# Odd attention: next position's first scores ahead of the last value products, output products beside the last positions, and a new order at both ends

## The reference

```python
for i in range(DEPTH):
    m = even_mixer(...) if i % 2 == 0 else odd_mixer(...)
    x = layer_norm(DEEPNORM_ALPHA * x + m, ln_mix_g[i], ln_mix_b[i])
    f = conv_ffn(x, w_up[i], conv_w[i], conv_b[i], w_down[i])
    x = layer_norm(DEEPNORM_ALPHA * x + f, ln_ffn_g[i], ln_ffn_b[i])
```

```python
z  = q @ k.T                                   # -inf where key >= query
sp = maximum(z, 0) + log1p(exp(-abs(z)))
a  = exp(z - (sum of sp from this key on to the query))
o  = a @ v
```

## Time and profile before

| | |
|---|---|
| median of 3 runs | 1261.15 us (1259.26 to 1261.15) |
| profiled execution | 1259.06 us, span 1257.2 us |
| TensorE busy | 1223.0 us, 97% of the span |
| VectorE, ScalarE, GpSimd busy | 630.4, 507.8, 554.2 us |
| odd attention, positions 0 to 7 | from 702.46 to 843.32 us |
| even attention, positions 0 to 7 | from 75.10 to 234.08 us |

### The profile page before, as it was taken

One profiled execution on the slowest core, in us unless ns is written; L12 is line 12 of the kernel. 1 busy time (PEld: TensorE's weight loads), 2 busy tenths in 40 slices (PEclk: granted clock), 3 DMA queues, 4 the chain that ended last, 5 costly groups with the idle time before them and its releaser, 6 DMA issues.

```text
span 1257.2 us, 17097 instructions
## 1 busy us (share of the span) xinstructions
PE 1223.0 (97%) x6274; PEld 1005.9 (80%) x6274; DVE 630.4 (50%) x992; ACT 507.8 (40%) x747; POOL 554.2 (44%) x242
## 2 busy tenths in 40 slices
PE   9999998999999999999999999989999999999996
PEld 8877776789888888888788777768988888888885
DVE  2045666276556665511370465553766666652226
ACT  3245565344333333322232556553533333342223
POOL 4534444343444444455614333314344444444553
PEclk9999999999999999999999999999999999999998
DMA  7221212123222222222222111112132222223211
GB/s 292 101 84 59 92 59 93 39 97 135 100 100 81 88 98 100 100 101 100 100 101 103 67 68 67 38 63 101 68 133 82 88 97 100 100 100 101 100 67 67
DMA packets 20022, 117.25 MB, mean 93 GB/s; under 512 B 2448, under 2 KB 2832, under 8 KB 7568
## 3 DMA queue, kind: packets, MB, share of 16 engines
q1 hardware_dynamic: 18400, 112.21, 24.8%
q10 hardware_dynamic: 1584, 4.51, 1.1%
HBM read 110.41 MB, written 2.10 MB: 89 GB/s over the span
## 4 chain that ended last, share of the span: by engine, by line
PE 87%; DVE 6%; ACT 3%; POOL 2%; issue 2%; DVEq 0%; ACTq 0%
PE bank L888 50%; PE bank L857 28%; POOL w_lo L244 2%; PE bank L940 2%; PE bank L967 1%; PE bank L954 1%; DVE probs L729 1%; PE bank L1024 1%; ACT w_hi L301 1%; PE bank L1005 1%; PE bank L1013 1%; PE bank L832 1%; DVE x L573 1%; DVE ln_mul L593 1%; DVE x L617 1%
## 5 line engine op out<-in xcount | busy, mean ns | idle before, releaser
L244 POOL TENSOR_TENSOR w_lo<-w_raw,w_hi 128x1024 fp32r<-128x1024 f32 x196 | 505.1, 2599 | 617.1 <-ACT w_hi L301 608.9
L888 PE MATMUL bank<-xt_hi,w_hi 128*128 128x512 f32 (+1 forms) x1056 | 397.0, 376 | 2.9 <-ACT v_all L331 1.7
L888 PE MATMUL bank<-xt_lo,w_hi 128*128 128x512 f32 (+1 forms) x1056 | 396.7, 376 | 0.0
L888 PE MATMUL bank<-xt_hi,w_lo 128*128 128x512 f32 (+1 forms) x1056 | 392.9, 372 | 0.0
L301 ACT ACTIVATE w_hi<-w_raw 128x2048 fp32r<-128x2048 f32 x97 | 185.3, 1910 | 208.5 <-PE bank L857 204.7
L888 PEld LDWEIGHTS bank<-xt_hi,w_hi 128*128 128x128 f32 x1056 | 198.9, 188 | 39.5 <-ACT v_all L331 2.4
L888 PEld LDWEIGHTS bank<-xt_lo,w_hi 128*128 128x128 f32 x1056 | 198.8, 188 | 39.1 <-issue 4.8
L888 PEld LDWEIGHTS bank<-xt_hi,w_lo 128*128 128x128 f32 x1056 | 198.7, 188 | 34.0
L857 PE MATMUL bank<-w_hi,a_hi 128*128 128x512 f32 x480 | 151.7, 396 | 2.9 <-POOL w_lo L244 1.9
L857 PE MATMUL bank<-w_hi,a_lo 128*128 128x512 f32 x480 | 149.0, 390 | 0.0
L857 PE MATMUL bank<-w_lo,a_hi 128*128 128x512 f32 x480 | 148.8, 390 | 0.0
(11 more groups left out here) (90 smaller groups left out, 1156.9 us busy)
## 6 DMA issues: line engine op xcount, KB each, us to landing
w_raw<-w_stream SPq DMA_DIRECT2D x97, 1024.0 KB, 4.8
x<-x_in SPq DMA_DIRECT2D x4, 512.0 KB, 7.1
gain<-ln_in ACTq DMA_DIRECT2D x4, 512.0 KB, 4.2
shift<-ln_in ACTq DMA_DIRECT2D x4, 512.0 KB, 6.3
qs<-qc SPq DMA_DIRECT2D x16, 128.0 KB, 2.1
ks<-kc SPq DMA_DIRECT2D x16, 128.0 KB, 2.0
out<-x SPq DMA_DIRECT2D x3, 512.0 KB, 2.6
w_raw<-w_stream SPq DMA_DIRECT2D x2, 512.0 KB, 5.9
```

Of the source, the lines that this page charges most:

```text
L244: pool.tensor_tensor(w_lo[slot(c)][:, part], w_raw[s][:, part], w_hi[slot(c)][:, part].bitcast(F32), ALU.subtract).then_inc(lo_ready, 1)
L888: mm = pe.matmul(out_bank[:, tok], w, m, start=n == 0, stop=n == len(todo) - 1)
```

## The change

1. `odd_position` of positions 0 to 6 sends `scores(0)` and `scores(1)` of the next position right behind its own `weigh(2)`, ahead of two fills, `weigh(3)` and the rest. They wait there for the next position's query and key. Position 0 alone (`first`) sends its own at its start. `share` becomes (10, 11, 15, 8, 2), so that all key products stand in front of `turn(2)`.
2. `odd_body` on ScalarE: the cast moves from the front of the position to behind `weight_part(0)`; the copy of the next keys moves from the end to ahead of `weight_part(3)`. On VectorE `break_stick(1)` goes ahead of `turn_out(0)`.
3. The output products of the first two steps are divided anew between the positions and what follows. Even layer: 6 in position 6, 30 in position 7, 60 behind (before: 0, 24, 72). Odd layer: 0, 48, 48. They now reach token tile 3 (banks 6 and 7) and need the bank that position 6 leaves, so a wait for `ot_lo` stands in front of it (`bank_free`). In odd position 7 all transposes use bank 4 (`turn_bank`), each waiting for the copy of the one before.
4. At the start VectorE makes the second token tile's remainder before it copies the second half of the first weights. In the last norm the last half's sum goes ahead of tile 2's value update.

The core of the diff (in `norm_out`, `norm` and `norm_last` the calls of `norm_root` are only written elsewhere, except for what point 4 says; `even_position` takes the same `filler` and `first` as the odd one):

```diff
@@ ScalarE, odd_body
-                for j in range(4):
-                    if j == 2 and before:
-                        out_heads(a, i - 1, (c - 1) % 2)
-                    if j == 0:
-                        heads(b + AT_QK + c + 2, it)
...
+                soft_part(0)
+                soft_part(1)
+                weight_part(0)
+                heads(b + AT_QK + c + 2, it)
+                if before:
+                    out_heads(a, i - 1, (c - 1) % 2)
+                weight_part(1)
+                soft_part(2)
+                turn_out(a, 1, 4 * i + 1, dense)
...
+                soft_part(3)
+                weight_part(2)
                 if dense:
                     act.wait_ge(w_used, b + AT_QK + i + 2)
                     act.activation(ka[(c + 1) % 2][:, :], bank[1][:, :], ACT.Copy).then_inc(a["k_ok"], 1)
+                weight_part(3)
+                turn_out(a, 3, 4 * i + 3, dense)
@@ TensorE, odd_position
-                share = (10, 11, 14, 9, 2) if dense else (6,) * 4 + (0,)
+                share = (10, 11, 15, 8, 2) if dense else (11, 11, 13, 9, 4)
...
-                    if j >= 2:
+                    if j >= 2 and dense:
                         pe.wait_ge(a["tev_v"] if j % 2 == 0 else a["tev_a"], 2 * i + j // 2)
+                    if j >= 1 and not dense:
+                        pe.wait_ge(a["tev_a"] if j % 2 == 0 else a["tev_v"], 2 * i + (j - 1) // 2 + 1)
...
+                if first:
+                    pe.wait_ge(a["q_ok"], i + 1)
+                    pe.wait_ge(a["k_ok"], i + 1)
+                    scores(0)
+                    scores(1)
...
                 weigh(2)
+                if dense:
+                    pe.wait_ge(a["q_ok"], i + 2)
+                    pe.wait_ge(a["k_ok"], i + 2)
+                    scores(0, 1 - par)
+                    scores(1, 1 - par)
                 fill(share[NT])
                 weigh(3)
@@ TensorE, even_position
-                share = (8, 8, 9, 9, 9, 3) if dense else (4, 4, 5, 5, 5, 1)
+                share = (8, 8, 9, 9, 9, 3) if early else (8, 8, 8, 3, 3) if dense else (3, 5, 7, 7, 6)
@@ TensorE, the layer
+                def bank_free(t, n, g):
+                    a = A[l]
+                    if (t, g) == (0, 0) and l == 0:
+                        pe.wait_ge(a["q_cp"], NPOS)
+                    if t == 3:
+                        pe.wait_ge(a["ot_lo"], NPOS - 1 + g)
...
+                if l == 0:
+                    beside = [(0, 0, 0)], [(0, 0, 1), (3, 0, 0), (0, 1), (3, 1, 0)]
+                    rest = [(1, 0), (2, 0), (3, 0, 1), (1, 1), (2, 1), (3, 1, 1)]
+                else:
+                    beside = [], [(0, 0), (2, 0, 1), (3, 0, 0), (0, 1), (2, 1, 1), (3, 1, 0)]
+                    rest = [(1, 0), (2, 0, 0), (3, 0, 1), (1, 1), (2, 1, 0), (3, 1, 1)]
...
-                position(b, 6, 0, True)
+                position(b, 6, 0, True, filler=outputs(beside[0], True))
+                position(b, 7, 0, False, filler=outputs(beside[1], True))
@@ VectorE, norm_last
                 norm_sum(i, 3, (0,))
+                norm_root(i, 2)
+                norm_sum(i, 3, (1,))
                 norm_out(i, 2)
-                norm_sum(i, 3, (1,))
                 norm_mul(i, 3)
@@ VectorE, start
             xt_rests(0, 0)
+            xt_rests(0, 1)
             dve.wait_ge(hi_ready, 1)
```

91 lines of the change are left out of this document (40 added, 51 removed).

## The result

The changed kernel took 1242.24 us (1241.35 to 1242.34), the kernel before 1261.15 us in the same job: a ratio of 0.9852, 95% interval 0.9835 to 0.9869. The forecast was 1243, range 1240 to 1249. The profiled execution took 1241.35 us (span 1239.5) for 1259.06 (span 1257.2) before, so 17.7 us less; the sum said 16.6.

What follows compares the result with a forecast made beforehand. TensorE sets the end, waiting 13.3 us for ScalarE's odd-layer exponentials. Gains 7.8 + 5.5 + 2.2 + 1.1 = 16.6 us off the profiled 1259.06 give 1242.5, forecast 1243 us; range 1240 to 1249.

Steps and rivals of the forecast that it cites:

- Part 1: Odd positions 0 to 6: next position's scores sent earlier, period from 17.81 to 16.6 us; gain 7.8 us.
- The 0.2 us between subtractions and third scan: Steady odd position: GpSimd's subtractions end at 11.0 us, VectorE's third scan starts at 11.2, so the moved cast costs nothing.
- Rival 1: Odd layer: steady gain smaller, wait up to 0.7 us at each third transpose; price 2 to 5 us, 1245 to 1248, chance 0.10.
- Part 2: Odd position 7: 48 output products as cover instead of 24, leaving 24 fewer behind it; gain 5.5 us.
- T: Time in us counted from the start of an odd position's four-block transpose, set as T = 0.
- The late output step: After odd position 7: the next output step's weights, cast and subtracted after the first step's last product, come 0.15 us late.
- Part 3: Even positions 6 and 7: output products as cover; gain 2.2 us, bounds 1.0 and 3.0.
- they cost nothing: gain 1.4: Even position 6: six output products, 1.4 us, run where TensorE sits idle anyway, so gain 1.4 us.
- a shorter idle time keeps the clock up: Even position 6: idle cut from 2.54 to near 1.3 us, clock stays full; 0.6 us more, or nothing if it falls.
- Part 4: Both ends of the kernel reordered: 0.6 us at the start, 0.5 at the end; gain 1.1 us.
- Rivals 2 and 3: 2: moved products wait too, cover gains 1.5 or 3 us, 1247 to 1250, chance 0.13; 3: slower, 1263 or above, 0.02.
- rival 3: Odd positions: scores' wait for the next keys blocks TensorE's queue if the key copy is late; 1263 us or above, chance 0.02.

Runs made afterwards that it cites:

- cast_later: Changed kernel with the odd positions' weight cast one place further back on ScalarE, behind the second exponential; 1251.81 us, ratio 0.9934.
- cast_front: Changed kernel with the weight cast back at the front of each odd position, scores still early; 1249.82 us, ratio 0.992.
- key_end: Changed kernel with the copy of the next keys back at the position's end, behind the last transposes' copy; 1247.92 us, ratio 0.9901.
- boundary_old: Changed kernel with early scores, cast move, key copy move and new fills undone together, cover and ends kept; 1253.56 us, ratio 0.9947.
- cover_old: Changed kernel with the old division of output products in both layers: none in position 6, 24 in position 7, 72 behind; 1249.58 us, ratio 0.992.
- even6_bare: Changed kernel with the six output products of even position 6 moved to the start of position 7; 1243.08 us, ratio 0.9862.
- scores_late: Changed kernel with each odd position's first two scores sent at its own start again, cast and key copy at their new places; 1251.73 us, ratio 0.9936.
- after_short: Changed kernel with GpSimd's subtractions in the odd attention cut to 256 of 1024 columns, for measuring only; 1241.22 us.
- ends_old: Changed kernel with the old order at both the start and the last norm; 1243.93 us, ratio 0.9874.
- odd6_cover: Changed kernel with six odd-layer output products moved from position 7 into position 6, ahead of its last transpose; 1242.85 us, ratio 0.9863.
- cast_later_short: Changed kernel with the odd weight cast behind the second exponential and GpSimd's odd-attention subtractions cut to 256 of 1024 columns, for measuring only; 1241.88 us, ratio 0.9853.

## Why the prediction was right

**Part 1 (7.8 said, 8.2 by the stage table).** The step that carried it, a slack of 1.5 us once the scores stand 1.03 behind the four-block transpose, held: they stand 1.11 behind it, the scan of 128 columns took 0.43 for the estimated 0.45, the exponential ends at 751.50 and the transpose goes at 753.11, 1.6 later. The period is 16.5 for 16.6. The 0.2 us between subtractions and third scan measured 0.3. Rival 1 stood on that margin. cast_later shows what lies behind it: once the scan is caught, positions 1 to 6 are each 1.2 us longer and position 7 is 1.8 longer, and with a stretch at half clock that makes 9.6 us; the 2 to 5 that I gave rival 1 were too low for a full catch. I had also called the cast's and the key copy's moves things that clear the way; cast_front and key_end show that each is needed for the whole gain. Position 0 gained its 0.6 by the terms named: waits of 0.11 and 0.58 for 0.2 and 0.7.

**Part 2 (5.5 said, 5.7).** Position 7 is 18.95 us for 19.1. The mis-sized term is its third wait, 0.22 for 0.7: the exponential was done at T + 12.99 as I had it (12.95), but TensorE reached the transpose at 12.77, not 12.25. The late output step measured 0.12 for 0.15. What the sum did not say is that part 2 needs part 1: in boundary_old, position 7's first transpose waits 1.37 us more, and undoing its moves costs 11.3 instead of 8.2. And part of the closeness of 18.95 to 19.1 is two errors that cancel: the wait is 0.5 shorter and TensorE's own work 0.3 longer (18.7 for 18.4).

**Part 3 (2.2 said, 2.5), right in the sum, wrong in what it gave the credit to.** I had 1.4 from the six products in position 6, 0.6 behind them from the clock and VectorE, 0.2 from position 7. cover_old, with the old even order at full clock, is 0.75 us shorter than before from the first scores of even position 6 to the first odd scores; there its position 6 is 18.39 for 19.06, so 0.67 of it is the half-rate stretch. That is the size that I gave the clock (0.6), and for the reason that I gave: at full clock TensorE then waits 0.46 us for VectorE's last copy. The rest of the stage's gain, 2.51 - 0.75 = 1.8 us, is the order of the products. even6_bare shows that it hardly matters that six of them stand in position 6 (about 0.1); what counts is that twelve products more are done by the end of position 7, 12 x 0.229 = 2.75, less the 0.9 by which that position grew (17.05 to 17.9: 17.43 to the end of its attention products, and two more products behind). The step that fails is "they cost nothing: gain 1.4". They did cost nothing (18.42 us with them, 18.39 without), but I priced that as a gain of its own without asking whether the same products would be nearly free one position later as well. The new wait for a_lo in position 7, 0.73 where I had 0.8, is its price; the one for w_lo (0.68) stood there before too (0.76). That a shorter idle time keeps the clock up is not borne out: it stayed full behind 2.53 us of idle in cover_old and fell behind 1.67 in cast_front and cast_later. Of the traces with the six products in position 6 the clock fell there in 3 of 11, of those without in 2 of 3, too few to tell. That it stayed up in both traces of the changed kernel may be luck. The Trainium skill's page "TensorE: Matmul & The Clock Gate", which I cited, says in its section "What's actually happening" that an idle array goes to half rate. The five even layers in which the clock fell behind 1.66 to 2.54 us of idle agree, and the others show that such idle time does not always do it. What decides it stays open.

**Part 4 (1.1 said, 1.2).** 0.4 at the start for 0.6, because x's transposes themselves began 0.2 later in this execution (7.36 for 7.15). That 0.4 is smaller than the scatter: the first scores of even position 6 come between 197.34 and 198.75 in the traces that have the changed kernel's start, and at 197.97 in before, so the start's share is argued from its one wait and not shown in the time. 0.8 at the end for 0.5: the last sum came 1.3 us earlier for 1.2, and from it to the end are 7.7 us for 7.2, since tile 2's update (1.28 us) now stands behind it; I had 0.7 for that.

**Rivals 2 and 3** did not come: no w_lo or a_lo wait in odd position 7 reached 1 us, and the wait for the next keys is never listed. key_end shows that rival 3's mechanism is real, 7 times 0.6 us once the copy stands one exponential later.

**The forecast itself.** 1243 lay 0.8 from the measured 1242.24, but it was put together from a profiled execution less the sum (1242.5) with a little added; the median less the sum would have been 1244.5. The sum was 1.1 short of the profiled pair, and 0.7 of that pair's 17.7 is before's stretch at half clock.

**Left open.** From the first scores of even position 6 to the odd scores, kernels with equal even code at full clock take 501.95 to 502.78 us. What comes and goes is a wait of TensorE at the transposes of x for the norm's output (L841 for L619): it is 0.4 to 0.5 us where the stage is longer (key_end 502.51, scores_late 502.42, after_short 502.78) and not listed where it is shorter (501.98, 501.96 and 502.06 in the two traces of the changed kernel and ends_old). In after_short the row reads as below. Why it comes in some traces only, no run shows.

```profile
PE bank L841 <- DVE x L619: 0.5, 2, 0.3
```

## What to carry to other kernels

When a chain of latency is longer than the work in front of it, look for work that can be sent ahead of the previous section's tail, and then follow every engine that the moved step used to keep apart: here the early scores paid in full only with the weight cast behind the first exponentials, which put GpSimd's long subtractions into the one gap between VectorE's scans. Before an idle stretch is filled with later work, ask whether that work would be free where it stands now; if so, filling gains next to nothing (0.1 us for six products in even6_bare, nothing in odd6_cover). Undo each edit of a package alone, and all together, before crediting one with the gain.

## What the runs showed of the hardware beyond the prediction

A VectorE scan whose input and output are in SBUF waits for the end of the GpSimd subtraction that runs when it starts, and then needs nearly its full time: clean 0.43, 0.69 and 0.96 us for 128, 256 and 384 columns, caught in steady positions 1.29 and 1.56 (before, cast_front), 0.96 and 2.02 (before, cast_front), and 1.97 to 2.32 (scores_late, cast_later). It waits for one subtraction only, not for the pair: in cast_front the first scan ends 0.26 us behind the middle of the pair, while the second subtraction runs.

TensorE's clock fell to 0.50 for 3.41 us in eight of the fourteen traces, once in each (leaving aside the fall at the end of the program): in the even layer in before, cast_front, cast_later, cast_later_short and even6_bare, in the odd layer in scores_late, key_end and cover_old, in the others not at all. In all five even cases it fell 208.21 us behind the clock's first rise. A stretch cost 0.67 us (even position 6 of before against cover_old) to 1.1 (cast_later_short against the changed kernel) and so can hide or feign a quarter to nearly a half of what part 3 is worth. A comparison at this size has to read the clock in both traces first.
